# Second mixer: per-head products over 64 rows in two row halves, and a float32r mask matmul

## The reference, cut to what matters

```python
s = jnp.einsum('bhclk,bhcsk->bhcls', q, k) * jnp.exp(log_d - m_row[..., None])   # log_d is -inf above the diagonal
inter = jnp.exp(m_inter - m_row)
num = jnp.einsum('bhcls,bhcsv->bhclv', s, v) + inter[..., None] * jnp.einsum('bhcvk,bhclk->bhclv', c_prev, q)
den = jnp.sum(s, axis=-1) + inter * jnp.einsum('bhck,bhclk->bhcl', n_prev, q)
h = num / jnp.maximum(jnp.abs(den), jnp.exp(-m_row))[..., None]
```

## Time and profile before

| | before |
|---|---|
| median of 3 runs | 1271.7 us (1267.66 to 1271.8) |
| span of the profiled execution | 1271.3 us |
| PE busy | 1221.5 us (96%) |
| DVE busy | 591.1 us (46%) |
| ACT busy | 350.6 us (28%) |
| GpSimd busy | 385.7 us (30%) |

### The profile page before, as it was taken

How to read it: one execution, slowest core, us unless ns; L and a number is a source line. 1 busy time by engine, 2 the same in 40 slices (tenths; PEclk the granted TensorE clock), 3 DMA queues, 4 the chain that set the end, 5 groups by cost and what they waited for, 6 DMA issues and landing times.

```text
span 1271.3 us, 16160 instructions
## 1 busy us (share of the span) xinstructions
PE 1221.5 (96%) x5803; PEld 976.2 (77%) x5803; DVE 591.1 (46%) x1009; ACT 350.6 (28%) x857; POOL 385.7 (30%) x202
## 2 busy tenths in 40 slices
PE   5989999999999889999999999999999999899997
PEld 5777777777777668888778877887788778688886
DVE  4546745845835851034243523462256235744443
ACT  5622513413413430001232123312331134301221
POOL 4433133132222223344223422242233322332000
PEclk9999999999989989999999999999999999999999
DMA  5111121021021033521112111211111110554222
GB/s 186 51 34 37 30 67 50 18 66 49 16 67 48 20 105 123 165 83 50 34 35 67 50 34 34 82 39 43 33 58 57 49 33 33 198 185 146 100 82 82
DMA packets 101657, 87.19 MB, mean 69 GB/s; under 512 B 4980, under 2 KB 91120, under 8 KB 101616
## 3 DMA queue, kind: packets, MB, share of 16 engines
q1 hardware_dynamic: 97008, 69.88, 18.4%
q10 hardware_dynamic: 4608, 16.78, 3.6%
HBM read 69.87 MB, written 16.78 MB: 68 GB/s over the span
## 4 chain that ended last, share of the span: by engine, by line
PE 79%; DVE 9%; ACT 5%; DVEq 3%; issue 2%; DMA 0%; ACTq 0%; SPq 0%
PE ps L522 61%; PE ps L790 2%; PE ps L795 2%; PE ps L791 2%; ACT probs L932 2%; DVEq L1231 2%; DVE row_max L1232 1%; PE ps L740 1%; PE ps L730 1%; DVE u_lo L1297 1%; PE ps L615 1%; PE ps L734 1%; PE ps L744 1%; PE ps L727 1%; DVE probs L1226 1%
## 5 line engine op out<-in xcount | busy, mean ns | idle before, releaser
L522 PE MATMUL ps<-hT_hi,w_hi 128*128 128x512 f32 x1216 | 483.5, 398 | 5.7 <-DVE hT_lo L1423 3.7
L522 PE MATMUL ps<-hT_lo,w_hi 128*128 128x512 f32 x1216 | 480.4, 395 | 0.0
L522 PE MATMUL ps<-hT_hi,w_lo 128*128 128x512 f32 x1216 | 479.1, 394 | 0.0
L478 POOL TENSOR_TENSOR w_hi<-w_raw,zero_col 128x1024 fp32r<-128x1024 f32 x85 | 165.9, 1952 | 758.1 <-PE ps L522 732.4
L522 PEld LDWEIGHTS ps<-hT_hi,w_hi 128*128 128x128 f32 x1216 | 230.6, 190 | 56.2 <-issue 5.5
L522 PEld LDWEIGHTS ps<-hT_hi,w_lo 128*128 128x128 f32 x1216 | 230.3, 189 | 47.5 <-issue 1.4
L522 PEld LDWEIGHTS ps<-hT_lo,w_hi 128*128 128x128 f32 x1216 | 230.6, 190 | 46.7 <-issue 2.1
L480 POOL TENSOR_TENSOR w_lo<-w_raw,w_hi 128x1024 fp32r<-128x1024 f32 x84 | 212.4, 2529 | 11.9
L932 ACT ACTIVATE probs<-probs,neg_max 128x128 f32<-128x128 f32 x128 | 49.9, 391 | 115.9 <-DVE neg_max L1238 115.9
L1041 ACT ACTIVATE dmat<-ps,tok_gate 128x128 f32<-128x128 f32 x64 | 20.1, 364 | 191.8 <-PE ps L734 163.3
L1368 DVE SCALAR_TENSOR_TENSOR s_T<-ps,dmat 128x128 f32<-128x128 f32 x64 | 15.6, 285 | 100.6 <-ACT dmat L1041 100.6
(11 more groups left out here) (217 smaller groups left out, 1430.0 us busy)
## 6 DMA issues: line engine op xcount, KB each, us to landing
w_raw<-in_w_in SPq DMA_DIRECT2D x68, 512.0 KB, 3.8
branch_a_scratch<-ev ACTq DMA_DIRECT2D x16, 512.0 KB, 2.6
xs<-in_x SPq DMA_DIRECT2D x8, 512.0 KB, 5.1
w_raw<-in_w_branch_attn SPq DMA_DIRECT2D x8, 512.0 KB, 3.7
ev<-branch_a_scratch ACTq DMA_DIRECT2D x8, 512.0 KB, 3.8
tanh_gm_scratch<-ev ACTq DMA_DIRECT2D x8, 512.0 KB, 2.6
w_raw<-in_w_branch_mlstm SPq DMA_DIRECT2D x8, 512.0 KB, 7.8
th<-tanh_gm_scratch SPq DMA_DIRECT2D x8, 512.0 KB, 3.6
```

Source lines behind the costliest of these rows:

```text
L478: nc.gpsimd.tensor_tensor(hi, src, zero_col[:].to_broadcast(list(src.shape)), ALU.add)
L522: mm = nc.tensor.matmul(ps[:, 2 * s + b, :], w[:, k, :], r_[:, k, b * BANK:(b + 1) * BANK], start=(r == 0), stop=(r == KT * TERMS - 1))
```

## The change

In the second mixer queries are no longer padded: `mq_pad` (two copies of 1024 columns, half zeros) becomes `mq_T` (one), filled by one DVE operation of 128 partitions. The two heads' key-query products become two matmuls over 64 rows each, head 0 on partitions 0 to 63, head 1 on 64 to 127, with 128 columns each, into two different banks (X[1] and X[2]). The same is done with queries times state (banks X[0] and X[3]). The transpose of the keys moves behind them, becomes the one that signals `m_scores`, and writes another place in its bank. The mask matmul takes a float32r identity and a float32r mask; the mask is first made in float32 (`causal_f`), then, behind one more drain of GpSimd, copied. ACT's line 1046 and DVE's lines 1368 and 1371 read the new places. The clearing of `mq_pad` is gone.

```diff
-        ident_b = sb("ident_b", [P, P], BF16)
+        ident_r = sb("ident_r", [P, P], F32R)
-        causal = sb("causal", [P, P], BF16)
+        causal = sb("causal", [P, P], F32R)
+        causal_f = sb("causal_f", [P, P])
...
-            [("raw_q", [P, T + 3]), ("raw_k", [P, T + 3]), ("mq_pad", [P, 2, T]), ("mk_T", [P, T]),
+            [("raw_q", [P, T + 3]), ("raw_k", [P, T + 3]), ("mq_T", [P, T]), ("mk_T", [P, T]),
...
+        qk_ps = [ps[:, X[1], 0:P], ps[:, X[2], 0:P]]
+        inter_ps = [ps[:, X[0], 2 * P:2 * P + MV + 1], ps[:, X[3], 0:MV + 1]]
...
-            triangle(causal[:], 0.0, NEG, 0, 1, -1)
-            nc.gpsimd.tensor_copy(ident_b[:], ident[:])
+            triangle(causal_f[:], 0.0, NEG, 0, 1, -1)
+            pool.drain()
+            nc.gpsimd.tensor_copy(causal[:], causal_f[:])
+            nc.gpsimd.tensor_copy(ident_r[:], ident[:])
...
                     nc.tensor.matmul(ps[:, X[0], 0:2 * P], ones_r[:], c_heads[:, :, tok], start=True, stop=False)
-                    nc.tensor.matmul(ps[:, X[0], 0:2 * P], ident_b[:],
+                    nc.tensor.matmul(ps[:, X[0], 0:2 * P], ident_r[:],
                                      causal[:].unsqueeze(1).to_broadcast([P, 2, P]), start=False, stop=True)
-                    nc.tensor.matmul(ps[:, X[1], 0:2 * P], mk_T[:, tok], mq_pad[:, :, tok], start=True, stop=True)
-                    mm = nc.tensor.transpose(ps[:, X[1], 2 * P:3 * P], mk_T[:, tok], ident[:])
+                    for j in range(2):
+                        rows = slice(64 * j, 64 * j + 64)
+                        nc.tensor.matmul(qk_ps[j], mk_T[rows, tok], mq_T[rows, tok], start=True, stop=True)
                     if c:
                         for j in range(2):
-                            mm = nc.tensor.matmul(ps[:, X[3], j * (MV + 1):(j + 1) * (MV + 1)], mq_pad[:, j, tok],
-                                                  state[:], start=True, stop=True)
+                            rows = slice(64 * j, 64 * j + 64)
+                            nc.tensor.matmul(inter_ps[j], mq_T[rows, tok], state[rows, :], start=True, stop=True)
+                    mm = nc.tensor.transpose(ps[:, X[1], P:2 * P], mk_T[:, tok], ident[:])
                     mm.then_inc(m_scores, 1)
...
-            for r in range(2):
-                V.memset(mq_pad[64 * (1 - r):64 * (1 - r) + 64, r, :], 0.0)
...
-                        for r in range(2):
-                            rows = slice(64 * r, 64 * r + 64)
-                            ins = V.scalar_tensor_tensor(mq_pad[rows, r, :], tanh_buf[rows, :], 1.0, z_buf[rows, :],
-                                                         ALU.add, ALU.mult)
+                        ins = V.scalar_tensor_tensor(mq_T[:], tanh_buf[:], 1.0, z_buf[:], ALU.add, ALU.mult)
```

More of the change, by code:

```diff
@@ L183, in build @@
         parity_sel = pT_cur[0:MH, 1, :]
-        (raw_q, raw_k, mq_pad, mk_T, v1, h_tok, gates, z_buf, tanh_buf, dmat, s_T, inter, k_w, state,
+        (raw_q, raw_k, mq_T, mk_T, v1, h_tok, gates, z_buf, tanh_buf, dmat, s_T, inter, k_w, state,
          c_heads, junk) = ml
@@ L1045, in mlstm_step @@
                         for j in range(2):
-                            ins = A(inter[:, j, :], ps[:, X[3], j * (MV + 1):(j + 1) * (MV + 1)], ACT.Copy,
+                            ins = A(inter[:, j, :], inter_ps[j], ACT.Copy,
                                     scale=tok_gate[:, c, 1, j:j + 1])
@@ L1367, in mlstm_step @@
                     for j in range(2):
-                        V.scalar_tensor_tensor(s_T[:, j, :], ps[:, X[1], j * P:(j + 1) * P], 0.25 * MK ** -0.5,
+                        V.scalar_tensor_tensor(s_T[:, j, :], qk_ps[j], 0.25 * MK ** -0.5,
                                                dmat[:, j, :], ALU.mult, ALU.mult)
                     for j in range(2):
-                        ins = V.tensor_scalar(k_w[:, j, :], ps[:, X[1], 2 * P + MK * j:2 * P + MK * (j + 1)],
+                        ins = V.tensor_scalar(k_w[:, j, :], ps[:, X[1], P + MK * j:P + MK * (j + 1)],
                                               tok_gate[:, c, 2, j:j + 1], 0.5, ALU.mult, ALU.mult)
```

## The result

| | before | after |
|---|---|---|
| median of the runs beside each other (17 each) | 1270.47 us (1267.66 to 1272.72) | 1273.37 us (1271.48 to 1275.21) |
| ratio to before, 95% interval | | 1.0019 (1.0013 to 1.0026) |
| span of the profiled execution | 1271.3 us | 1272.5 us |

The changed kernel is 0.2% slower, some 2.4 us (1.7 to 3.3): no change by the 0.5% bound of the prediction, but one clear of the runs' spread. The forecast was + 1.0 us, with 0.6 to 1.2 for its sum, which lies under the measured interval: the time that was forecast, 1272.7 us, came out closer than the difference did. The busy times hardly differ from the earlier trace rows, although PE has 64 more instructions.

A forecast was written before the change was run, and what follows sets the result against it. PE was taken as the bound, through the first group of small products: 28 x 0.00 + 4 x 0.22 = 0.9 us, taken as 1.0, on 1271.3 plus 0.4 gave 1272.7 us; range 1266 to 1286.5.

The forecast's parts named there:

- PE sets the time: Second mixer: PE is busy 131.97 of 132 us; each 0.1 us in a chunk counts 32 times.
- Mask in float32r: First group's mask matmul: its step takes 0.31 us where it had 0.12, plus 0.19 per chunk.
- Row halves together: Query-key and state products: both halves run at once, 0.64 us with c > 0, 0.42 with c = 0.
- Rival 1: Row halves run in turn: 13.2 us more, time 1285.9; chance 20 in 100.
- the prediction's sign: Row-half product, line 730: four records in two pairs 0.11 us apart, second head's within 0.02 of the first's.
- Transpose to second dense matmul: End of the first group, after the change back to 128 rows: 0.40 us.
- The change of rows: First group: a change in the weights' number of rows costs 0.09 us and exposes a load of 0.11.
- Rival 2: The change between 128 and 64 rows costs nothing: 10.9 us less, time 1261.8; chance 8.
- Sum: First group: 1.66 against 1.66 us with c > 0, 1.44 against 1.22 with c = 0; 1.0 taken overall.
- DVE: Query filling: one 128-partition operation per pair, between 1.2 and 3.4 us, nearest row 1.7; covered, zero gain.
- Start: Constants at kernel start: some 0.3 us plus a drain, under 2 us of cover; at most 0.5 if uncovered.
- The two rules: Skill rules: loads overlap only on other rows (some 1282, 3 in 100); float32r may load fast (1269.5, chance 5).

The follow-up runs named there:

- e1: Kernel before with only the float32r mask and identity, products still padded; ratio to before 1.0027, + 3.4 us.
- e7: Changed kernel with both heads' key-query and state products on partitions 0 to 63, head 0's standing in for head 1's; ratio to before 1.013, 1286.54 us.
- e5: Kernel before with the block of ones and per-head row values on 128 rows instead of 40, added rows zero; ratio to before 0.9937, - 8.0 us.
- e4: Changed kernel with the mask matmul ahead of the 40-row matmul; ratio to before 0.9912, 11.2 us under before.
- e6: Changed kernel with the block of ones and per-head row values on 128 rows instead of 40; ratio to before 0.9921, - 10.0 us.
- e3: Changed kernel with an unused buffer added so that the mixer's buffers lie where they lay before; ratio to before 1.001.
- e2: Changed kernel with the bfloat16 mask and identity of before, row halves kept; ratio to before 0.998, - 2.5 us.

## Why the prediction was right

The path, the waits and the prices of the steps were right. The difference itself was not as near as the time: measured + 2.4 us, forecast + 1.0. That 1272.7 lies 0.7 us from the measured 1273.37 is partly luck, since its base, the median of three runs (1271.7), lay 1.2 us above the median of 17 (1270.47). Nor is the 0.4 us between span and median a property of the kernel: in every run on record, time and span differ by 1.7 to 1.8 us.

Point by point, by its own steps:

- *PE sets the time, every tenth of a us in a chunk counts 32 times.* Shown: the sums of starts lie within the measured interval in seven of eight kernels.
- *Mask in float32r, 0.31 instead of 0.12.* 0.32 measured; alone (e1) + 0.10 a chunk.
- *Row halves together, 0.64 us with load and change.* 0.65 measured. This step rested on column halves alone and could have failed; e7 shows the other case at its forecast price. Rival 1 is out. (The first pairs start 0.21 us apart and not the 0.11 of the prediction's sign, because the first record holds its exposed load; the sum had that load.)
- *Transpose to second dense matmul, 0.40.* 0.40 measured.
- *The change of rows costs 0.09 and exposes the load.* e5 takes both changes away and nothing else, and gets back 0.275 us of the 0.29 per group; e4 gets 0.39 of 0.42. Rival 2 (128 to 64 rows for nothing) is out by e6 and by the 0.32 us behind the mask.
- *Sum.* Here is the one size that was off: for c > 0 I had 1.66 against 1.66, and the starts say 1.676 against 1.660. The 0.016 are roundings of my prices. To a thousandth, from the mask to the first row half there are 0.318 us instead of 0.31, and the passes take 0.646 instead of 0.64, as the second head's records start 0.006 behind the first's; the other steps are within 0.002. I had allowed for 0.01 a group. 28 times it is 0.45 us, and with 4 x 0.24 the groups cost 1.4 us, where I said 1.0.
- *What I had no term for:* the dense slice behind a group with c > 0, 0.031 us each, together 0.9 us. It is the rest to 2.3 us, and over a third of the difference. Its cause stays open. It is not the placement (e3), not the float32r mask alone (e1 has 2.738), not row halves as such (e4 has them and 2.738 with c > 0, though 2.767 with c = 0; e5 has none and 2.767), and not that the halves run together (e7 has 2.769). In the fast slices the distances between starts are 0.226 to 0.227 us from the third to the last but one. In the slow ones most distances up to the fifth, sixth or ninth are 0.228 to 0.236, in a few fixed patterns. Two such starts of the changed kernel (0.236 to a thousandth):
```profile
612.11 0.40 PE L528 MATMUL ps<-hT_hi,w_lo 128*128 128x512 f32 x1
612.35 0.39 PE L528 MATMUL ps<-hT_hi,w_hi 128*128 128x512 f32 x1
```
  No run was made that would show where it comes from.
- *DVE.* The one operation of 128 partitions took 1.2 us once and 3.4 in the median, my upper bound, instead of the nearest row's 1.7:
```profile
L1348 DVE SCALAR_TENSOR_TENSOR mq_T<-tanh_buf,z_buf x4: 1226/3415/3424, 574.9 to 973.7; 128x1024 f32<-128x1024 f32 x4
```
  The keys' operation, which the change does not touch, went from 1.7 to 3.3:
```profile
L1350 DVE SCALAR_TENSOR_TENSOR mk_T<-tanh_buf,mk_T x4: 1224/3282/3282, 585.7 to 984.6; 128x1024 f32<-128x1024 f32 x4
```
  Both are covered as said: no wait of PE for queries or keys appeared.
- *The wait at line 752.* Unchanged, answering to the earlier trace rows:
```profile
  DVE h_tok L1408: 1.9, 4
```
- *Start.* GpSimd's last constant now comes at 9.29 + 0.22 = 9.51 us, 0.5 later than in the earlier trace rows; PE waited for the transfer until 10.3 all the same. No cost.
```profile
9.29 0.22 POOL L479 TENSOR_SCALAR_AFFINE_SELECT pair_mask<-pair_mask 8x32 f32<-8x32 f32 x1
```
- *The two rules.* Within one half, the second pass starts 0.21 us behind the exposed first one and the following ones 0.11 apart, in the changed kernel (both halves in 0.65 us) and in e7 (all eight in one half in 1.09): loads for the same rows do hide under a running pass here too. This is against the rule of the Trainium skill, "TensorE: Matmul & The Clock Gate", section "The mechanism", that a weight load overlaps a running matmul only when it goes to other rows; the same section of the Trainium skill also lets a load for a background weight buffer run ahead, and no run here shows whether that is what happens. The float32r identity does not load fast: its record is 0.19 us beside 0.10 for bfloat16, and e1 pays 0.10 a chunk. The same page of the Trainium skill, section "Weight-path perf modes", would have it fast if float32r counted as "not FP32".

## What to carry to other kernels

Splitting a product into row halves does run both at once and halves its passes, but here each change between the full array and a part of it cost about 0.09 us and laid the next weight load bare. So one product in halves between full matmuls lost (e2, c = 0: 0.14 us a group), two in a row gained little (c > 0: 0.09); the gain comes when everything that uses part of the rows stands together (e4), or when the lone partial matmul is filled up to 128 rows with zeros (e5). Look for a matmul with few rows in the middle of full ones: here it had been costing 8 us. The price of a weight type depends on whether its load is hidden: float32r instead of bfloat16 cost 3.4 us behind a change of rows and, by the steps of e4 and e6, nothing in the stream. The two heads' results went to different banks throughout; halves that write one bank were not tried.

## What the runs showed that I had not expected

- The 40-row matmul leaves the other half of the array free: in e4 a pass of 64 rows, by the reading above the second head's, starts 0.01 us behind it (738.51 and 738.52).
- A slice of 13 identical dense matmuls can differ by 0.03 us (2.738 to 2.770) with the instructions ahead of it, in the same way in nearly every chunk.
- A DVE operation over 128 partitions took 1.2 us in its fastest case and 3.4 in the median, the same two times as operations of half as many partitions had the earlier trace rows. No run tried what slows it, but the trace shows it beside GpSimd's split of a weight tile (line 486). Where GpSimd starts 0.05 us earlier, DVE's record ends 1.08 us behind GpSimd's end; where DVE starts 0.04 earlier, DVE takes its 1.2 and GpSimd 3.4 instead of 2.4:
```profile
707.82 2.39 POOL L486 TENSOR_TENSOR w_lo<-w_raw,w_hi 128x1024 fp32r<-128x1024 f32 x1
707.87 3.42 DVE L1348 SCALAR_TENSOR_TENSOR mq_T<-tanh_buf,z_buf 128x1024 f32<-128x1024 f32 x1 [1.94 <-ACT tanh_buf L1001]
```
```profile
574.87 1.23 DVE L1348 SCALAR_TENSOR_TENSOR mq_T<-tanh_buf,z_buf 128x1024 f32<-128x1024 f32 x1 [2.18 <-ACT tanh_buf L1001]
574.91 3.42 POOL L486 TENSOR_TENSOR w_lo<-w_raw,w_hi 128x1024 fp32r<-128x1024 f32 x1
```
  All four of these operations fit this, as does the keys' (line 1350): whichever of the two engines starts second runs longer by roughly what the first still needs.
